# A hybrid mixer block on one core: delta-rule pieces at other places of TensorE's queue, rotary halves exchanged by ScalarE

## What is computed

```
q, k, v: short convolution, silu; q, k scaled to unit length per head
g = -A softplus(a + bias);  beta = sigmoid(b)                      # per token and head
S_t = exp(g_t) (I - beta_t k_t k_t^T) S_{t-1} + beta_t k_t v_t^T;   o_t = S_t^T q_t
# in chunks: G = cumsum(g), A = strict_lower(beta k k^T exp(G_i - G_j))
#   u, w = (I + A)^-1 [beta v, beta k exp(G)];  v_new = u - w S
#   o = (q exp(G)) S + (q k^T * decay) v_new;   S = exp(G_last) S + k_dec^T v_new
rq, rk = apply_rope(rq), apply_rope(rk)      # t1 c - t2 s | t1 s + t2 c on the halves of a head
o_ret = retention(rq, rk, rv), normed per head with mean and variance, times silu(rg)
x = x + g1 * (concat(o_gdn, o_ret) @ w_out);  x = x + g2 * swiglu(...)
```

## Time and profile before

| | us |
|---|---|
| median of 3 runs (3381.61 to 3382.19) | 3382.01 |
| the profiled execution | 3379.65 |
| its span | 3377.5 |
| TensorE busy (16746 matmuls) | 3306.6 |
| GpSimd busy | 1516.2 |
| ScalarE busy | 1368.7 |
| VectorE busy | 1189.8 |

### The profile page before, as it was taken

One profiled execution on the slowest core, in us unless ns is written; L12 is line 12 of the kernel. 1 busy time (PEld: TensorE's weight loads), 2 busy tenths in 40 slices (PEclk: granted clock), 3 DMA queues, 4 the chain that ended last, 5 costly groups with the idle time before them and its releaser, 6 DMA issues.

```text
span 3377.5 us, 45592 instructions
## 1 busy us (share of the span) xinstructions
PE 3306.6 (98%) x16746; PEld 2775.3 (82%) x16746; DVE 1189.8 (35%) x1878; ACT 1368.7 (41%) x1976; POOL 1516.2 (45%) x1114
## 2 busy tenths in 40 slices
PE   6999999999999999999999999999999999999998
PEld 4778888888898888888888888888888888888887
DVE  6763775211131115444125111411035452161104
ACT  4444445443244323247225442443333374244423
POOL 2333112554445454545544554455445545445444
PEclk8999999999999999999999999999999999999999
DMA  6332001222222222322222222222222222222222
GB/s 268 129 143 78 1 1 63 100 93 100 94 92 96 99 94 82 106 94 100 94 88 93 94 98 97 79 106 94 99 85 96 100 94 100 94 82 99 97 95 100
DMA packets 90034, 322.22 MB, mean 95 GB/s; under 512 B 9776, under 2 KB 12208, under 8 KB 89776
## 3 DMA queue, kind: packets, MB, share of 16 engines
q1 hardware_dynamic: 88576, 316.71, 26.9%
q10 hardware_dynamic: 1328, 3.67, 0.3%
HBM read 318.24 MB, written 2.10 MB: 95 GB/s over the span
## 4 chain that ended last, share of the span: by engine, by line
issue 40%; POOL 31%; PE 23%; DVE 3%; DMA 1%; POOLq 1%; ACT 1%; SPq 0%; DVEq 0%; ACTq 0%
POOL w_lo L476 31%; PE ps L534 4%; PE ps L535 4%; PE ps L539 4%; DMA ada_first<-ada 1%; PE ps L839 1%; DVE inverse_span L1975 1%; PE ps L1102 1%; PE ps L1097 1%; PE ps L1095 1%; PE ps L554 1%; PE ps L961 1%; PE ps L1121 0%; PE ps L1125 0%; PE ps L1119 0%
## 5 line engine op out<-in xcount | busy, mean ns | idle before, releaser
L476 POOL TENSOR_TENSOR w_lo<-raw,w_hi 128x512 fp32r<-128x512 f32 x1086 | 1484.1, 1389 | 1709.2 <-ACT w_hi L1269 1709.1
L1269 ACT ACTIVATE w_hi<-raw 128x1024 fp32r<-128x1024 f32 x543 | 575.3, 1060 | 1436.9 <-PE ps L539 901.8
L535 PE MATMUL ps<-acts,w_hi 128*128 128x512 f32 x2776 | 1080.0, 389 | 0.0
L534 PE MATMUL ps<-acts,w_hi 128*128 128x512 f32 x2776 | 1079.9, 389 | 0.0
L539 PE MATMUL ps<-acts,w_lo 128*128 128x512 f32 x2776 | 685.6, 389 | 0.0
L539 PEld LDWEIGHTS ps<-acts,w_lo 128*128 128x128 f32 x2776 | 521.1, 188 | 108.1
L534 PEld LDWEIGHTS ps<-acts,w_hi 128*128 128x128 f32 x2776 | 521.2, 188 | 108.0
L535 PEld LDWEIGHTS ps<-acts,w_hi 128*128 128x128 f32 x2776 | 521.1, 188 | 107.9
L2297 DVE TENSOR_TENSOR tmp<-tmp,ps 128x512 f32<-128x512 f32 x110 | 75.6, 687 | 781.8 <-PE ps L539 728.3
L2300 DVE TENSOR_TENSOR acts<-tmp,acts 128x512 f32 x110 | 117.6, 1069 | 154.2 <-ACT acts L1628 154.2
L1095 PE MATMUL ps<-acts,w_hi 128*128 (+1 forms) x440 | 171.2, 389 | 0.0
(11 more groups left out here) (385 smaller groups left out, 3966.2 us busy)
## 6 DMA issues: line engine op xcount, KB each, us to landing
raw<-stream SPq DMA_DIRECT2D x543, 512.0 KB, 3.2
ada_behind<-ada SPq DMA_DIRECT2D x32, 512.0 KB, 3.4
ada_first<-ada SPq DMA_DIRECT2D x8, 1024.0 KB, 12.6
X<-x_in ACTq DMA_DIRECT2D x1, 2048.0 KB, 8.5
out<-X SPq DMA_DIRECT2D x16, 128.0 KB, 1.9
xin<-x_in ACTq DMA_DIRECT2D x2, 768.0 KB, 6.8
xin<-x_in SPq DMA_DIRECT2D x2, 768.0 KB, 9.0
rope_sb<-rope SPq DMA_DIRECT2D x1, 1280.0 KB, 9.8
```

The lines of the kernel that those rows point to most:

```text
L476: last = nc.gpsimd.tensor_tensor(w_lo[:, slot, part, :], raw[:, slot % RAW, part, :], f32(w_hi[:, slot, part, :]), ALU.subtract)
L534: mm(o, w_hi[:, s, k, :], xh, start=start, stop=False, skip_group_check=True)
L535: mm(o, w_hi[:, s, k, :], xl, start=False, stop=False, skip_group_check=True)
L1269: A(w_hi[:, s, :, :], raw[:, s % RAW, :, :], ACT.Copy).then_inc(s_hi, 1)
```

## The change

**Roped items.** ScalarE copies the projection out as before and also the upper half to the lower partitions and the lower to the upper, into a second buffer. The sine table has the sign in it. VectorE multiplies both and adds; the exchange on TensorE goes, with its constant matrix. The sum of squares of item 0 now stands behind item 3.

**Gates.** Two more products give the cumulated gates also as rows (`gate_cols` with `cst1`); VectorE splits them in a high and a low part and spreads them by head (`head_rows`, f32r). The rows of a step are then one f32r product of 512 columns for each direction, with a selecting column (`chosen`), in place of four fp32 products. The exponentials of the gates stand ahead of the retention's on ScalarE, and three copies of turned tiles ahead of `Dsum` on VectorE.

**Delta rule.** The pieces are cut in halves or directions and stand either between the first and the second products (`under_copies`) or behind the second (`under_merges`), at levels given by tables for each step. The state's products with the queries stand behind level 6 and between the two directions' new values. `ret_squares` stands at the end of steps 0 and 1, the squares of the means are GpSimd's. VectorE's and ScalarE's side work follows by direction; from step 1 on `both_matrices` (and from step 2 on the second negative matrix) stands behind level 6, and the unit matrices of step 0 come early. GpSimd's mask products wait for the turned blocks of their step (`s_xt`). Several buffers change places. The first products of the output projection wait for the last outputs only where they use their banks.

```diff
+ROWS_AT, KEYS_AT, STATE_AT = (1, 1, 3, 3, 3, 0), (3, 4, 5, 5, 5, 0), (0, 2, 3, 3, 3, 1)
+ABOVE_AT, BELOW_AT, BOTH_AT = (3, 5, 5, 5, 5, 0), (5, 5, 6, 6, 6, 0), (5, 6, 6, 6, 6, 0)
...
             for s in range(NCC, NC):
                 for d in range(2):
-                    pool.wait_ge(s_na[d], s + 1)
+                    pool.wait_ge(s_xt, 5 * s + 1)
...
-                if i >= 2:
-                    kind, h = items[i - 2]
...
+                for j in () if i < 3 else (0, 1) if i == 3 else (i - 2,):
+                    kind, h = items[j]
+                    if kind in NORMED:
+                        pe.wait_ge(s_squares, n_aux[j])
...
                         g = tok[:, 0, :]
+                        for d in range(2):
+                            mm(ps[7][:, 256:256 + P], gate_cols[d][:, :], cst1[:, d, :], start=(d == 0), stop=(d == 1))
...
-                    for h in range(H):
-                        col = 24 * d + 4 * order[d][s] + h
-                        last = mm(ps[4 * d + 3][:, h * P:(h + 1) * P], tok[:, 0, col:col + 1].to_broadcast([P, P]),
-                                  cst1[:, d, :], start=True, stop=True)
-                    last.then_inc(s_rows, 1)
...
+                    elif s:
+                        pe.wait_ge(s_na[d], s)
+                        pe.wait_ge(s_gS[d], s - 1)
+                    row = NC * d + order[d][s]
+                    mm(ps[4 * d + 3][:, :], chosen[:, row:row + 1].to_broadcast([P, P]), head_rows[:, :],
+                       start=True, stop=True).then_inc(s_rows, 1)
...
+            def under_copies(s, lev):
+
+                if s >= NCC and lev in (1, 2) and s < NC - 1:
+                    keys_queries(s, lev - 1, 0)
+                if s == NC - 1 and lev > 2:
+                    keys_queries(s, (lev - 3) // 2, (lev - 3) % 2)
+                if s and lev - STATE_AT[s] in (0, 1):
+                    keys_state(s, lev - STATE_AT[s], 0)
+                if s < NC - 1:
+                    if lev == ROWS_AT[s] and s < NCC:
+                        decay_rows(s + 1)
+                    if lev == KEYS_AT[s]:
+                        key_products(s + 1, 0, 0)
+                        key_products(s + 1, 0, 1)
+                    if lev == KEYS_AT[s] + 1:
+                        key_products(s + 1, 1, 1)
+                if s == 0 and lev in (2, 4):
+                    ret_sums(lev - 2)
+
+            def under_merges(s, lev):
+
+                if s >= NCC and lev in (1, 2) and s < NC - 1:
+                    keys_queries(s, lev - 1, 1)
+                if s and lev - STATE_AT[s] in (0, 1):
+                    keys_state(s, lev - STATE_AT[s], 1)
+                if s < NC - 1 and lev == KEYS_AT[s]:
+                    key_products(s + 1, 1, 0)
+                if lev == ROWS_AT[s] and s >= NCC:
+                    decay_rows(s + 1)
+                if s >= NCC and lev == 6:
+                    state_queries(s, 0)
...
                     last.then_inc(s_vp[d], 1)
+                    if s >= NCC and d == 0:
+                        state_queries(s, 1)
+                if s < 2:
+                    ret_squares(2 * s)
...
+                        parts = [(slice(0, CTX), C[:, 0:CTX]), (slice(CTX, TOK), L)] if kind == "rk" else [(slice(0, LAT), L)]
+                        for cols, bank in parts:
+                            A(b[:, cols], bank[:, :], ACT.Copy)
+                            for a in range(2):
+                                last = A(c[half[a], cols], bank[half[1 - a], :], ACT.Copy)
+                        last.then_inc(s_pread, 1)
...
+                        k = ROWS_AT[s]
+                        first = 1 if s >= NCC else 4
+                        if lev in (first, first + 1):
+                            decayed_keys(s, lev - first)
+                        if lev in (k, k + 1):
+                            differences(s + 1, lev - k)
+                        if s + 1 >= NCC and lev in (k + 1, k + 2):
+                            query_factors(s + 1, lev - k - 1)
+                        if lev == k + 2:
+                            decays(s + 1)
...
+                    if s in (1, 2) and lev == 1:
+                        ret_variances(2 * (s - 1))
+                    if NCC <= s < NC - 1 and lev in (1, 2):
+                        masked_queries(s, lev - 1)
+                    if s == NC - 1 and lev in (4, 6):
+                        masked_queries(s, lev // 2 - 2)
+                    if s and lev - STATE_AT[s] in (1, 2):
+                        right_side(s, lev - STATE_AT[s] - 1)
...
+                    if s < NC - 1:
+                        if lev == ABOVE_AT[s]:
+                            negative_matrix(s + 1, 0)
+                        if lev == BELOW_AT[s]:
+                            negative_matrix(s + 1, 1)
+                        if lev == 6:
+                            units()
+                        if lev == BOTH_AT[s]:
+                            both_matrices(s + 1)
```

More of the change, by code:

```diff
@@ L780, in keys_state @@
                         pe.wait_ge(s_go[d], s - NCC)
-                    for h in range(H):
-                        last = mm(ps[4 * d + 2][:, h * P:(h + 1) * P], kT[:, h, c * P:(c + 1) * P],
-                                  gts[s % 2][d][11][:, h, :], start=True, stop=True)
-                    last.then_inc(s_ks, 1)
+                    if s in (1, 2):
+                        pe.wait_ge(s_hvar, 2 * s + d - 1)
+                for h in HEADS[half]:
+                    last = mm(ps[4 * d + 2][:, h * P:(h + 1) * P], kT[:, h, c * P:(c + 1) * P],
+                              gts[s % 2][d][11][:, h, :], start=True, stop=True)
@@ L786, in _, with state_queries @@
+            def state_queries(s, d):
+                pe.wait_ge(s_qd, 2 * (s - NCC) + d + 1)
+                qd, S = (gts[s % 2][d][i] for i in (6, 11))
+                for h in range(H):
+                    mm(ps[4 * d + 2][:, h * P:(h + 1) * P], S[:, h, :], qd[:, h, :], start=(h == 0), stop=False,
+                       skip_group_check=True)
             pe.wait_ge(s_rv, 4)
@@ L809, in _ @@
                 if s == NCC + 2:
-                    key_products(0)
+                    for d in range(2):
+                        for half in range(2):
+                            key_products(0, d, half)
             def ret_sums(first):
@@ L1533, in _ @@
                     last.then_inc(s_vn[d], 1)
-            for j in range(1, H):
-                head_operand(j)
+            head_operand(1)
             for d in range(2):
@@ L1544, in _ @@
                 A(hq[:, h, :], ogdn[:, h, :], ACT.Square).then_inc(s_hsq, 1)
+            for j in range(2, H):
+                head_operand(j)
             for j in range(H, 2 * H):
@@ L2153, in _ @@
                         add_rows(s, d, c, ogdn, ps[b + 2]).then_inc(s_go[d], 1)
-            head_low(2)
-            head_low(3)
+            head_low(1)
+            for j in range(2, H):
+                head_result(j)
+                head_low(j)
             for j in range(H, 2 * H + 1):
```

323 lines of the change are left out of this document (141 added, 182 removed).

## The result

| | before | changed |
|---|---|---|
| median of 4 runs | 3382.1 (3381.61 to 3383.94) | 3351.6 (3350.41 to 3354.18) |
| the profiled execution | 3379.65 | 3351.78 |
| its span | 3377.5 | 3349.9 |

The changed kernel is faster: ratio 0.991, 95% interval 0.9893 to 0.9927, 30.5 us between the medians. Forecast were 3352 and a gain of 30.0.

What follows compares the result with a forecast made beforehand. TensorE's queue was taken to bound the projections and the stretch from 580 us, and a loop no engine bounds alone the delta-rule steps. Gains of 31.7 less 1.7 leave 30.0: 3349.7 profiled, median 3352 us, range 3343 to 3366.

Steps and rivals of the forecast that it cites:

- Turns of the roped projections: In the projections: the turning products leave TensorE's queue, where it never waits, a gain of 8.6 us.
- Rival (2): Projections give nothing back: ScalarE's dearer cross copies or late first root stall TensorE at k items; 3361 us, chance 0.06.
- ScalarE's copies of halves: In the projections: a half copy of 512 columns on 64 partitions takes 0.59 us, at most twice that.
- Before the loop: Gate, decay-row and unit-matrix work ahead of the steps: 0.45 us added, 1.3 and 0.7 saved.
- A full step: Steps 2, 3 and 4 of the delta rule: 27.0 us against 30.93, with TensorE's own 25.5 as floor.
- The predicated copy: On VectorE behind level 6: takes 0.74 us instead of 1.85, because GpSimd's mask products now wait for the turn behind it.
- Reserve for changes of kind: In the steps: f32r rows among fp32 products cost 0.29 us per change of kind, six times, 1.7 off the gain.
- The gain is kept: Behind step 5, from the output projection on: TensorE is busy again without waits, so nothing won is lost.
- Rival (4): The gain is lost behind 540 us, where the output projection waits for weights or heads; 3382 us, chance 0.03.

## Why the prediction was right

The mechanism was right: TensorE's queue got shorter by what was removed, and the loop's waits were filled by pieces cut to size. The total (30.0) was met to 0.5 by the medians (30.5), which is in part luck, as the end of this section shows; the profiled pair gives 27.9. Step by step:

- *Turns of the roped projections*, 8.6: the work removed is right (8.55 with the waits gone). What the step missed is what the late sum pushes. I walked it to the squares of the second k item, which fit: they end at 94.42 and TensorE wants them at 94.97, though with 0.55 to spare and not 1.5. I did not walk it to the conditioning rows, which stand behind the next k item's convolution in VectorE's queue. Rival (2) named the wrong wait, and its price is 2.0 us, or 3.5 to 3.6 where half clock follows, not 8.6.
- *ScalarE's copies of halves*: 0.60 for 64x512 and half of 0.77 for 64x256, as for 128 partitions; the assumed 0.59 holds. A whole rk evacuation takes 2.97 (105.93 to 108.90), more than the 2.4 to 2.6 of the sum, and is still hidden.
- *Before the loop*, 2.11 from the gate item on, 1.6 forecast.
- *A full step*, 27.0: measured 26.40 (26.89 in step 2). Of the 0.6 too much, half is the first period with the lateness of the first merge, 3.25 where the walk had 2.75 and 0.8 on top; that lateness is 0.33 to 0.57 in starts (0.18 of recorded idle). The rest is in the periods 2 and 3, 2.68 and 3.25 instead of 2.75 and 3.45, and in level 5 to level 1, 13.99 instead of 14.05.
- *The predicated copy* at 0.74 in all steps: so it is (0.73 or 0.74), and the run with the early mask shows that GpSimd beside this and the unit matrices costs 2.2 a step at these places, twice what I had priced.
- *Reserve for changes of kind*, 1.7: not needed, as the rows' 0.91 shows. With the merges it makes the loop's excess: 23.7 gained in the steps and behind them, 21.5 in the sum, 19.8 with the reserve.
- *"The gain is kept"*: in the profiled execution it was not, by 4.9 us. Rival (4) had the place and the kind of wait, at a sixth of its price. The rest ranges from 2812.2 to 2817.3 over twelve profiled executions; the queues of before show 2812.4 and 2814.8, those of the changed kernel 2812.6 to 2817.3 (2812.2 with the square moved). These overlap, so how much the change itself costs there is not settled by the totals.

For the wait at the first norm the theory of the experiments (no effect of the change) is doubtful. The block under the fifth split took 3.3 to 3.4 us in both kernels with the queues of before and in the run with fp32 decay rows, and 4.1 to 5.5 in all nine others. Exactly in these nine a 16 KB packet of the queue "instruction" lies within the block's time, as shown above for the changed kernel. It comes 8.5 to 8.6 us behind the start of the next chunk in eight of the nine and 9.7 in the run with whole pieces. In the kernel before it comes at 11.7, when the block has landed, and in the other two there is none from 5.8 before the start of that chunk to 18.7 behind it. The profiles count 94 such packets in each of the nine and 95 in each of the three. So where the packet falls goes with the kernel and hardly varies between executions, which speaks for an effect of the change. That the packet is what delays the block is not shown: it is a correlation over twelve executions, and no run moved it alone.

The total came out right also because these errors cancel. In the profiled execution a loop 3.9 better than forecast and a start of the loop 0.5 better met projections 1.9 worse and 4.9 lost in the rest. The median execution of before is 2.5 longer than its profiled one, and with that the medians come to 30.5; where those 2.5 lie no trace shows.

## What to carry to other kernels

When a sum or a wait moves in one queue, walk every instruction that stands behind its consumer on the other engines, the small ones that serve something else above all: here four copies of two partitions cost 2.0 to 3.6 us, up to an eighth of what the change had won. In a chain of dependent engines, cut a side piece to the size of each gap (3.7 us here), and see which engine's work runs beside which: moving GpSimd's product from beside two VectorE copies was worth 7.0 by the medians. A piece moved out of a stalled level gains nothing where the levels that take it up have no idle time. Compare starts stretch by stretch, from a common event rather than from the span's start, since an effect of a few us in one stretch is hidden in the medians by another that varies by five. And look at the DMA view of a late block for packets that are not the kernel's own.

## What was not expected of the hardware

- A copy of fp32 from SBUF to SBUF beside GpSimd's product took 1.83 us for two of 128x512 instead of 0.76, as hard hit as the predicated copy (1.70 against 0.74). GpSimd's own product took 1.38 instead of 1.27.
- After TensorE had idled 1.8 us in the projections, the granted clock fell to 0.5 for a stretch in six of seven executions, at a cost of 1.5 to 1.6 us. It fell after 1.7 us at the start of step 0 in two (that step then takes 28.3 instead of 27.3), and after 1.8 us in the norm in the changed kernel. At the same places in the other executions it stayed at 1.00, behind a wait of 2.4 in the norm (the run with whole pieces) too. So a short wait can cost nearly twice its length, and need not.
- A weight block of 512 KB took 3.3 to 3.4 us from issue to use in three executions and 4.1 to 5.5 in the nine in which one 16 KB "instruction" packet fell into its transfer.
